# A two-layer decoder kernel: rotation tables and position-bias lines in one opening block, the lines' store issued in the differential attention

## The reference, cut to what matters

```
for i in range(2):                       # first model
    u = rmsnorm(x) @ w_in[i]
    y_a = stick_breaking_attention(...)  # 8 heads
    y_b = differential_attention(rope(q, cos, sin), rope(k, cos, sin), v, lam)   # 4 heads
    x = x + (sigmoid(gate_a) * y_a @ w_br_a + sigmoid(gate_b) * y_b @ w_br_b) @ w_o
    x = x + hierarchical_moe(rmsnorm(x)) # top 2 of 32 experts
    x = x + (p @ w_ple) * sigmoid(rmsnorm(x) @ w_ple_gate)
x = rmsnorm(x)
# second model, one layer: its windowed and block attention add, to each logit of head h,
# rel_bias_2[bucket(query - key), h]
```

## Time and profile before

| | |
|---|---|
| median of 3 runs | 2600.31 us |
| profiled execution, its own time | 2599.12 us |
| its span | 2597.3 us |
| PE busy | 2326.9 us, 90% |
| DVE, ACT, POOL busy | 38%, 22%, 16% |
| mean granted PE clock | 0.96 |
| DMA, mean | 155 GB/s |
| bytes written to HBM | 30.15 MB |

### The profile page before, as it was taken

The page is one execution under the profiler, slowest core; times in us unless marked ns, Lnnn a source line. Parts: engine busy times, 40 slices in busy tenths (PEclk is TensorE's granted clock), DMA queues, the critical chain, the costliest instruction groups (busy, mean ns, idle before and its releaser), DMA issues. The chain is left out here.

```text
span 2597.3 us, 29809 instructions
## 1 busy us (share of the span) xinstructions
PE 2326.9 (90%) x11776; PEld 1716.6 (66%) x11776; DVE 995.3 (38%) x1726; ACT 575.6 (22%) x1177; POOL 410.4 (16%) x404
## 2 busy tenths in 40 slices
PE   4899999688888898999968987699999999999998
PEld 3666788544446666678844444587776888788886
DVE  3344543511115444553341113444564333432234
ACT  2242420311112243340121112313433001200011
POOL 1101021112211101112111211111111121111111
PEclk9999999889999899999979999899999999999999
DMA  5402223699973311223489995232321333233321
GB/s 162 115 25 62 64 86 124 263 365 415 413 305 131 107 41 43 60 69 105 194 310 413 415 415 205 65 106 74 86 84 45 99 98 106 82 97 97 98 98 65
DMA packets 291553, 402.98 MB, mean 155 GB/s; under 512 B 31306, under 2 KB 230730, under 8 KB 273478
## 3 DMA queue, kind: packets, MB, share of 16 engines
q1 hardware_dynamic: 276444, 373.31, 40.9%
q0 software_dynamic: 10176, 16.81, 1.8%
q10 hardware_dynamic: 4778, 10.76, 1.5%
HBM read 388.99 MB, written 30.15 MB: 161 GB/s over the span
## 5 line engine op out<-in xcount | busy, mean ns | idle before, releaser
L130 PE MATMUL banks<-h_split,w_high 128*128 128x512 f32 x2624 | 836.5, 400 | 7.9 <-DVE w_low L182 5.6
L130 PEld LDWEIGHTS banks<-h_split,w_high 128*128 128x128 f32 x2624 | 485.7, 190 | 114.7 <-issue 8.2
L130 PE MATMUL banks<-h_split,w_low 128*128 128x512 f32 x1312 | 517.5, 394 | 0.0
L171 POOL CAST w_high<-w_raw 128x1024 fp32r<-128x1024 f32 (+1 forms) x264 | 275.8, 1045 | 1523.5 <-PE banks L130 1336.7
L182 DVE TENSOR_TENSOR w_low<-w_raw,w_high 128x1024 fp32r<-128x1024 f32 (+1 forms) x264 | 316.7, 1199 | 518.4 <-POOL w_high L171 518.2
L130 PEld LDWEIGHTS banks<-h_split,w_low 128*128 128x128 f32 x1312 | 248.6, 189 | 55.6
L130 PE MATMUL banks<-w_high,op_split 128*128 128x512 f32 x736 | 231.2, 394 | 1.0 <-DVE mg_part L1102 1.0
L1637 PE MATMUL banks<-expert_ring,ex_xsT 128*64 128x256 f32 x1472 | 178.1, 397 | 20.2 <-DMA expert_ring<-in_w_exp_up 17.3
L130 PEld LDWEIGHTS banks<-w_high,op_split 128*128 128x128 f32 x736 | 138.2, 188 | 33.8 <-DVE mg_part L1102 2.2
L1637 PEld LDWEIGHTS banks<-expert_ring,ex_xsT 128*64 128x64 f32 x1472 | 106.5, 143 | 77.8 <-DMA expert_ring<-in_w_exp_up 18.8
L130 PE MATMUL banks<-w_low,op_split 128*128 128x512 f32 x368 | 144.8, 393 | 0.0
(11 more groups left out here) (395 smaller groups left out, 2730.0 us busy)
## 6 DMA issues: line engine op xcount, KB each, us to landing
w_raw<-in_w_in SPq DMA_DIRECT2D x142, 512.0 KB, 4.2
expert_ring<-in_w_exp_gate SPq DMA_DIRECT2D x46, 1024.0 KB
expert_ring<-in_w_exp_up SPq DMA_DIRECT2D x46, 1024.0 KB
expert_ring<-in_w_exp_down SPq DMA_DIRECT2D x46, 1024.0 KB
w_raw<-in_w_gu SPq DMA_DIRECT2D x44, 512.0 KB, 4.1
region<-in_w_exp_gate SPq DMA_DIRECT2D x20, 1024.0 KB
region<-in_w_exp_up SPq DMA_DIRECT2D x20, 1024.0 KB
region<-in_w_exp_down SPq DMA_DIRECT2D x20, 1024.0 KB
```

The costliest lines, as they stand in the source:

```text
L130: last = nc.tensor.matmul(out, left, right, start=(start and n == 0), stop=(stop and n == 2), skip_group_check=True)
L171: self.nc.gpsimd.tensor_copy(self.high[:, i % self.SPLIT, 0:n], self.raw[:, i % self.RAW, 0:n]).then_inc(self.high_ready, 1)
```

## The change: what it does

- The two opening blocks become one, `opening_tables`. SP issues the five small tables after the positions and ahead of x. PE's products stand beside DVE's angle chain; DVE makes the lines after the angles; ACT takes the cosine first, then the sine, then loads the square-root table. The barrier between the blocks goes.
- The store of the lines leaves the opening. ACT issues it in `differential`, after its table load, ahead of the wait for lambda's products. As this is in the loop's body, it is issued in both passes, with the same bytes.
- SP waits for it at the end of its part of `combine_experts` in each pass, no longer in `final_norm`.

```
-            rotary_tables(k, t, k.cosT, k.sinT, load_start(k, t, opening, raw), raw)
-            bias_lines(k, t["rel_bias_2"], lines, line, k.bias_stored)
+            opening_tables(k, t, k.cosT, k.sinT, line, load_start(k, t, opening, raw), raw)
             clear_sems(k)

 def opening_tables(...):                       # sync
             sp.dma_start(freq[:], t["c_rope_freq"]).then_inc(landed, 16)
+            sp.dma_start(table[:], t["rel_bias_2"]).then_inc(line_landed, 16)
+            ... hot, apart, kinds, hidden ...
             start.issue(sp)
                                                # vector, after the angle chain
+            for n in (0, 1):
+                dve.wait_ge(multiplied, 2 * n + 2)
+                ... hidden = near * kinds[0] + hidden; line = far * kinds[1] + hidden ...
                                                # scalar
-            for n, dst in enumerate((sinT, cosT)):
+            for n, dst in enumerate((cosT, sinT)):
                 act.wait_ge(reduced, n + 1)
                 nc.scalar.activation(dst[:], dst[:], ACT.Sin)
+            act.preload_act_table_set("sqrt_and_others")

 def bias_lines(...):
-            act.wait_ge(line_ready, 2)
-            nc.scalar.dma_start(lines, line[:].unsqueeze(1).to_broadcast([BIAS_HEADS, P, LINE])).then_inc(stored, 16)

 def differential(...):                         # scalar
         act.preload_act_table_set("natural_log_exp_and_others")
+        lines, line = kept_lines
+        nc.scalar.dma_start(lines, line[:].unsqueeze(1).to_broadcast([BIAS_HEADS, P, LINE])).then_inc(sem["lines_stored"], 16)
         act.wait_ge(sem["lam_step"], 2)

 def combine_experts(...):                      # sync
             st.loads(sp, 0, st.RAW)
+            sp.wait_ge(lines_stored, 16)

 def final_norm(...):                           # sync
-            if wait_for is not None:
-                sp.wait_ge(wait_for, 16)
```

More of the change, by code:

```diff
@@ L597, in _, with opening_tables @@
             low_result(pairs - 1)
-def rotary_tables(k, t, cosT, sinT, start, raw):
+def opening_tables(k, t, cosT, sinT, line, start, raw):
     nc = k.nc
@@ L620, in _ @@
             sp.dma_start(freq[:], t["c_rope_freq"]).then_inc(landed, 16)
+            sp.dma_start(table[:], t["rel_bias_2"]).then_inc(line_landed, 16)
+            sp.dma_start(hot[:], k.t["c_bucket_hot"]).then_inc(line_landed, 16)
+            sp.dma_start(apart[:], k.t["c_bucket_apart"]).then_inc(line_landed, 16)
+            sp.dma_start(kinds[:], k.t["c_bias_kinds"]).then_inc(line_landed, 16)
+            sp.dma_start(hidden[:], k.t["c_hidden"]).then_inc(line_landed, 16)
             start.issue(sp)
@@ L632, in _ @@
                 nc.gpsimd.tensor_copy(dst[:], raw[:, n, :])
+        @block.tensor
+        def _(pe):
+            pe.wait_ge(line_landed, 80)
+            for n in (0, 1):
+                for m, buckets in enumerate((hot, apart)):
+                    nc.tensor.matmul(k.ps[0:BIAS_HEADS, 2 * n + m, 0:half], table[:], buckets[:, n * half:(n + 1) * half],
+                                     start=True, stop=True).then_inc(multiplied, 1)
         @block.vector
@@ L642, in link, with angles @@
                 dve.wait_ge(step, done[0])
[L644 to L647, removed]
+            def angles(n, quarter, dst):
                 u = turn[:, n, :]
@@ L658, in _, with differential @@
                 nc.vector.tensor_scalar(dst[:], dst[:], lim, -lim, ALU.min, ALU.max).then_inc(reduced, 1)
+            dve.wait_ge(landed, 32)
+            link(nc.vector.tensor_copy(ang[:], pos_i[:]))
+            link(nc.vector.tensor_scalar(ang[:], ang[:], freq[:], None, ALU.mult))
+            angles(0, 0.25, cosT)
+            angles(1, 0.0, sinT)
+            for n in (0, 1):
+                dve.wait_ge(multiplied, 2 * n + 2)
+                part = slice(n * half, (n + 1) * half)
+                nc.vector.scalar_tensor_tensor(out=hidden[:, part], in0=k.ps[0:BIAS_HEADS, 2 * n, 0:half], scalar=kinds[:, 0:1],
+                                               in1=hidden[:, part], op0=ALU.mult, op1=ALU.add).then_inc(near_ready, 1)
+                dve.wait_ge(near_ready, n + 1)
+                nc.vector.scalar_tensor_tensor(out=line[:, part], in0=k.ps[0:BIAS_HEADS, 2 * n + 1, 0:half],
+                                               scalar=kinds[:, 1:2], in1=hidden[:, part], op0=ALU.mult, op1=ALU.add)
         @block.scalar
         def _(act):
-            for n, dst in enumerate((sinT, cosT)):
+            for n, dst in enumerate((cosT, sinT)):
                 act.wait_ge(reduced, n + 1)
                 nc.scalar.activation(dst[:], dst[:], ACT.Sin)
-def differential(k, ctx, room, st, lams, gain, lam_init, keep, cosT, sinT, raw, yT, early):
+            act.preload_act_table_set("sqrt_and_others")
+def differential(k, ctx, room, st, lams, gain, lam_init, keep, cosT, sinT, raw, yT, early, kept_lines):
     nc = k.nc
@@ L2894, in _, with final_norm @@
                                                op0=ALU.mult, op1=ALU.mult).then_inc(final_done, 1)
-def final_norm(k, tag, gain, out=None, wait_for=None):
+def final_norm(k, tag, gain):
     nc = k.nc
@@ L2909, in _ @@
             sp.dma_start(g[:], gain.partition_broadcast(P)).then_inc(landed, 16)
-            if wait_for is not None:
-                sp.wait_ge(wait_for, 16)
-            if out is not None:
-                for t in range(NT):
-                    sp.wait_ge(normed, t + 1)
-                    sp.dma_start(out[0, t * P:(t + 1) * P, :], k.x[:, t, :]).then_inc(stored, 16)
-                sp.wait_ge(stored, 16 * NT)
         @block.scalar
@@ L2986, in second_layer, with first_layer @@
         second_half(k, st, m, op, fd, t["g_ffn_2"][0], t["g_final_2"], hiddenT, silu, final_g, out)
-def first_layer(k, t, i, scratch):
+def first_layer(k, t, i, scratch, line, lines):
     nc = k.nc
@@ L3029, in first_layer @@
             with ExitStack() as room:
-                attention, yb_ready, early_ready = differential(
+                attention, yb_ready, early_ready, lines_stored = differential(
                     k, ctx, room, st, [t[n][i] for n in ("lam_q1", "lam_k1", "lam_q2", "lam_k2")], t["g_subln"][i],
-                    t["c_lam_init"][i], t["c_keep"][i], k.cosT, k.sinT, da_raw, ybT, early)
+                    t["c_lam_init"][i], t["c_keep"][i], k.cosT, k.sinT, da_raw, ybT, early, (lines, line))
         assert -(-nc.sbuf_base // 32) * 32 == ring_base
@@ L3078, in program @@
         with nc.Fori(0, DEPTH) as i:
-            first_layer(k, t, i, (xn_rows.ap(), y_rows.ap()))
+            first_layer(k, t, i, (xn_rows.ap(), y_rows.ap()), line, lines)
             clear_sems(k)
         first_stack.close()
-        final_norm(k, "fn", t["g_final"], wait_for=k.bias_stored)
+        final_norm(k, "fn", t["g_final"])
         second_layer(k, t, lines, out)
```

23 lines of the change are left out of this document (13 added, 10 removed).

## The result

| | before | after |
|---|---|---|
| median of the runs | 2600.25 us (2599.10 to 2600.74, 4 runs) | 2616.98 us (2616.54 to 2621.49, 4 runs) |
| span of the profiled execution | 2597.3 us | 2614.7 us |

The account below looks back on a forecast made before the run. PE, busy 90% of the span, was taken as the bound, with loads slowed beside the store. Opening -9.1, stick-breaking -17.7 and differential attention +41.8 gave +15.0 us: 2615.3 us, range 2598 to 2625.

Parts of the forecast that it names:

- The opening: Merged opening block: DVE's lines end at 16.8 us, POOL's casts at 16.9, loop starts at 18.1; gain 9.1 us.
- POOL's casts end at 16.9: Opening: five loads issued ahead of x move POOL's casts by up to 2.3 us, from 14.60 to 16.9.
- Stick-breaking: First pass: without the store beside it, it runs as in the second pass; gain 17.7 us.
- The differential attention: Both passes: the store delays small loads, pieces 19 and 20 and DVE's work behind them; 20.9 us lost per pass.
- the small loads: Differential attention: last four issued after the store; first takes 10.3 us, the others 5.0; lambda's inputs at 223.5, not 213.8.
- The half clock's 2.0 us: Differential attention: PE's wait before the transpose of step 0 brings half clock after it, costing 2.0 us more per pass.
- PE's waits: Differential attention: PE idle some 9 us for the copies of v and 7 for the difference of step 0.
- Rival A: Differential attention hides the store, if a column piece beside it lands in under about 7 us: 2573.5 us; chance 13%.
- The sentence on turns beside this rival: By the skill's whole-packet queue switching, 64 rows wait for 4 to 7 store turns; the 13.34 us speak against it.
- Rival B: Differential attention: the store's lead does not hold up the small loads; 14.3 us a pass, 2602.1 us; chance 10%.
- C: Differential attention: a third split, of piece 21, also becomes late; 26 us a pass, 2625 us; chance 7%.
- no more is lost there: Differential attention: the split of piece 21 ends at 264.9 us, before DVE's shifted next work at 266.4; no further loss.

Follow-up runs that it names:

- e2: Kernel before with only the merged opening, the store issued once at the opening's end and nothing in the loop: 2593.5 us, ratio 0.997.
- e6: Changed kernel with the store issued in stick-breaking, behind ACT's logarithm of step 1, in both passes, not in the differential attention: 2573.4 us.
- e4: Changed kernel, store in the same place, DVE's splits of pieces 19, 20 and 21 moved behind work of steps 0, 1 and 2: 2591.6 us.
- e5: Changed kernel with each pass storing half of the 128 copies: 2585.4 us, ratio 0.994.
- e8: Changed kernel with SP issuing piece 19 ahead of the seven small loads of lambda: 2596.5 us, ratio 0.998.
- e3: Changed kernel with the store issued two lines later, after the exponential of lambda's products, in both passes: 2571.1 us, ratio 0.989.
- e7: Changed kernel with a store of 16 of the 20 lines, the last four heads left out: 2639.3 us, ratio 1.015.
- e9: Changed kernel with the twenty lines on every fourth partition of an 80-partition tile: 2617.9 us, ratio 1.007.

## Why the prediction was right

Right in sign, in mechanism and within 2 us in the median, with two sizes off. That it came so near is in part luck: the two passes together cost 5.0 us more than forecast, and 0.6 us in the opening and 2.0 us that nothing explains took half of it back.

- **The opening**, forecast -9.1, measured -9.7. The step "POOL's casts end at 16.9" is wrong: they ended at 15.11, since they began 1.9 us later than before (forecast 2.3) and took 0.29 to 0.51 us each, for 0.51 to 0.78 before; I had moved their end by the whole issue time of five loads. DVE's chain, forecast 16.8, measured 16.54, was the end. e2, with the store's issue at the end, gives 8.4.
- **Stick-breaking**, forecast -17.7, measured -17.7. e6 and e2 show the reason from two sides: a store at 70 us costs nothing there, one at 16 us costs all 17.7.
- **The differential attention**, forecast +20.9 a pass, measured 23.7 and 23.1. Mechanism and order were as told: small loads, pieces 19 and 20, DVE's order. The sizes, from the stage's start: lambda's products 20.65 us (forecast 18.7), piece 19 taken at 34.7 (32.1), piece 20 at 48.4 (45.4), transposes 21.7 us late (18.9). The step that was mis-sized is the small loads: I had SP's issue at 0.38 us each and the wait in the queue behind it; the issue itself took 2.1 to 2.3 us. The store was also issued at once and not behind the table load, so its first rows went 1.6 us after the stage's start (54 rows by 180 us) and not 2.7 us. Each piece then took 13.65 to 14.06 us for 13.3. The half clock's 2.0 us was right for the last wait. PE ran at half clock after each of the three waits, 7.3 us in all, but what it lost after the first two lies inside the 21.7 us.
- **PE's waits**: forecast 9 us for the copies and over 7 for the difference; measured 6.46 and 7.80, and 3.59 for piece 17, whose split DVE holds behind lambda's products. I had read this split as free. In this kernel it adds nothing to the sum, since the copies wait for piece 19 either way and PE's wait for them is only the shorter for it. It is the earliest sign in the profile, and in e4, e5 and e8 it is the largest wait that is left.
- **The sum** for the span, forecast +15.0, measured +17.4: +5.0 in the stage, -0.6 in the opening, and the 2.0 us that are not explained. The medians are 16.7 apart.
- **Rival A** (hidden) was wrong for this place, and e3 shows it right 9 us later in the same stage. Its condition, a piece beside the store in under 7 us, was not met there either (13.6 us). The condition was wrong: what counts is whether the piece is due. The sentence on turns beside this rival is wrong too. It takes each turn of the store as one row; were the store's turns as long as SP's, 64 rows would wait for as many rows of the store, and the 13.34 us would not speak against that rule. The single packets in the trace of the kernel before do: from 76.0 to 79.3 us ten or eleven rows of SP's queue begin in every 0.208 us, and the rows begun by the two queues never differ by more than five, where turns of nine rows and more on ten engines should show. **Rival B** (small loads not held up) is excluded by the wait of 11.80 us. **C** lies above.
- **Pieces 21 and later**: "no more is lost there" was right. In the changed kernel DVE splits piece 21 at 237.83 us without a wait, and in e3 too.

## What to carry to other kernels

- A long store on another queue costs by what stands at its head. List the loads that the same DMA engines must bring within its duration, with the time at which somebody really waits for each; two lines further on in ACT's program were worth 46 us here.
- A row's price beside the store (0.208 us an engine here) is only paid by rows that are issued once it runs. Look for small loads of 128 rows in the first microseconds behind it.
- An in-order engine that takes up a late piece ahead of ready work passes the delay on: moving three splits, with no DMA changed, gave back 25 us. What it left was in good part the same fault one step earlier: the split of piece 17 behind lambda's products, with 3.6 to 6.2 us of PE's time a pass in e4, e5 and e8.

## What the runs showed of the hardware

- ACT issued the store beside its own table load (177.38 and 177.35 us), not after it.
- SP's issue of a small load takes 0.33 to 0.38 us. Beside a store on ten engines the last four took 2.1 to 2.3 us each, and 4.4 to 4.5 beside one on sixteen (e7). Without a store beside them just one of the seven was long: 2.27 us in the kernel before, 1.70 in e3.
- More engines made the store no faster: 195 rows in 5 us on sixteen, 240 on ten. The counts of e7 and e9 fit 48 to 49 rows in 5 us for each group of source partitions that is being read, an account that no run tested by itself. Sixteen equal shares were the worst case for every other queue.
- A DMA share of 0.65 in the stage of e3 cost PE nothing; 0.68 in the changed kernel stood beside 16.5 us of idle time. The share alone does not tell.
